# Zero matmuls ahead of the first data, and the identity loaded before the norm weights

## The chip, the cores and the metric

The kernel runs on one core of a Trainium2 chip. The metric is the time of one launch in microseconds (us), the median of three runs. The core has an engine for matrix products (TensorE, in the profile PE, and PEld for its loads of the stationary operand), three engines that work element by element (VectorE is DVE, ScalarE is ACT, GpSimd is POOL) and one that issues loads (SyncE, SP). Each has its own list of instructions and waits for the others on semaphores. Loads move data by 16 DMA engines which all queues share.

## The reference, cut to what matters

Four layers run one after the other over 256 tokens of width 2048, all in 32 bit floats: two hybrid layers, then a banded one and a grid one.

```python
def first_block(x, ...):
    for l in range(DEPTH):                       # DEPTH = 2
        x = hybrid_layer(x, pre_norm_g[l], post_norm_g[l], w_in[l], ...)
def hybrid_layer(x, pre_g, post_g, w_in, b_in, w_out, ...):
    h = rms_norm(x, pre_g)
    p = split_columns(h @ w_in + b_in)           # 2048 columns in, 6992 out
    ... four kinds of attention on the pieces of p ...
    return x + rms_norm(mix @ w_out, post_g)
def second_block(x, ...):
    x = _layer_ab(...); x = _layer_c(...)        # x + (attention(norm(x) @ w_in) * silu(z)) @ w_out
    return _rmsnorm(x, ln_f)
```

Only the very first product, `h @ w_in` of the first layer, is near the change. Its weights w_in are read from memory once, and nearly all of the kernel's TensorE time is spent in such products.

## The kernel before, in words

**Precision.** A product of 32 bit floats is made of three matmuls in the one-pass type fp32r: every operand is split in a high part (`w_hi`, `xt_hi`, written by ACT) and the rest (`w_lo`, `xt_lo`, written by DVE), and PE adds hi·hi, hi·lo and lo·hi. In the first slot these are lines 1552, 1553 and 1554, in all later ones 1503 to 1505.

**Chunks.** The columns of a weight matrix are worked off in slots of 512 columns. A slot has four chunks (0 to 3 for the first slot, 4 to 7 for the second, and so on), each of four pieces of 128 rows by 512 columns, 1 MB in all. Chunks go round a ring of three buffers `raw[0..2]`: SP loads a chunk when DVE has split the chunk that had the buffer before (`raw_free`, line 425), then ACT makes `w_hi` (line 641), DVE makes `w_lo` (line 975), then PE multiplies 24 matmuls.

**The start.** The first four chunks are worked piece by piece, since everything waits for data there. SP issues the first 256 columns of x, the pieces of chunk 0, and so on, x and pieces in turn (lines 432 and 435). ACT's queue issues two small loads: `gT`, the norm weights (line 854), and the identity matrix, which is the first 128 columns of `cst` (line 855). PE waits for the identity and the head of x, and transposes x (`x_cols_t(0)`, line 1535: four transposes into one bank of PSUM). ACT scales the turned columns by `gT` into `xt_hi` (lines 660 and 661), and splits two pieces (line 866). DVE writes `xt_lo` (line 1330) and `w_lo` (line 1322). Then `first_slot` starts: six matmuls of a piece, four transposes of the next columns of x (`x_cols_t(1)`), six matmuls, four transposes, and so on. From chunk 3 on, the ring decides when a load may be issued. SP also loads the rest of `cst` (line 448), and POOL, once that is in, the biases and small weights of the layer (lines 515 to 535) by its own queue.

**Order.** The order on each engine is written out by hand: the program of an engine is its instruction list. Nothing else decides it.

## Time and profile before

| | us |
|---|---|
| median of three runs | 1887.13 |
| the three runs | 1882.69, 1887.13, 1889.14 |
| the profiled execution, its own time | 1885.34 |
| its span, first to last instruction | 1883.3 |
| TensorE (PE) busy in it | 1857.6 |
| VectorE busy | 1011.1 |
| ScalarE busy | 859.5 |
| waits of PE for DVE's `w_lo` after the first slot, 5 times | 8.3 |
| wait of PE for the first data | 5.3 |

A row of the timeline gives the start, the duration, the engine, the line of the kernel, the operation, what it writes and reads with its shape, and in brackets how long the engine had been idle and what ended that. A row of the windows gives busy time of each engine in a stretch, then the clock that TensorE was granted as a share of its full 2.4 GHz (0.50 is 1.2 GHz), the busy share of the 16 DMA engines, and GB/s. The share can read slightly above 1. Before the first change of clock that the profiler recorded this column reads 1.00 in any case; there the distance between starts of equal matmuls tells the level.

### The profile page before, as it was taken

Reading aid. Unit: us, or ns where it says so; the run is one execution under the profiler, and the core shown is the slowest. Engines: PE = TensorE matmul, PEld = TensorE weight load, DVE = VectorE, ACT = ScalarE, POOL = GpSimd, SP = SyncE. Lnnn points to the kernel's source line nnn. Section 1 sums busy time; section 2 is a strip of 40 time slices with the busy share of each in tenths; the row PEclk is TensorE's granted clock in tenths of the full one; section 3 lists DMA queues with packets and bytes.
Section 4 is the critical chain, followed back from the end, with each engine's and each line's share of the span. In section 5 each row is a group of like instructions: output and inputs, shape, how many; then the busy total and the mean of one; then the engine's idle time right before and its main releaser. Section 6 shows DMA issues by size and latency. Waiting matters only on the chain.

```text
span 1883.3 us, 22540 instructions
## 1 busy us (share of the span) xinstructions
PE 1857.6 (99%) x9566; PEld 1590.7 (84%) x9566; DVE 1011.1 (54%) x987; ACT 859.5 (46%) x1066; POOL 163.2 (9%) x168
## 2 busy tenths in 40 slices
PE   8999999999999999999999999999999999999998
PEld 6889988898788998889878888888888888888886
DVE  5545454474663455457465555455455555555544
ACT  5344443464543445346445443354354434435443
POOL 2300011000340001000020000010000101100011
PEclk9999999999999999999999999999999999999999
DMA  9665555455566455446556555455556555456553
GB/s 313 201 193 153 157 189 169 145 182 190 191 203 205 144 172 191 149 140 205 170 176 197 183 192 189 161 184 175 182 179 200 179 167 184 146 172 201 174 184 112
DMA packets 187156, 338.99 MB, mean 180 GB/s; under 512 B 6848, under 2 KB 48688, under 8 KB 186160
## 3 DMA queue, kind: packets, MB, share of 16 engines
q1 hardware_dynamic: 181536, 316.89, 51.8%
q0 software_dynamic: 5232, 20.59, 3.9%
q8 instruction: 76, 1.25, 0.3%
q14 instruction: 24, 0.20, 0.0%
q10 hardware_dynamic: 288, 0.07, 0.0%
HBM read 335.43 MB, written 2.10 MB: 179 GB/s over the span
## 4 chain that ended last, share of the span: by engine, by line
PE 92%; DVE 3%; ACT 2%; DMA 1%; issue 1%; ACTq 0%; DVEq 0%
PE acc L1503 27%; PE acc L1505 27%; PE acc L1504 27%; PE bank L1656 3%; DVE w_lo L975 2%; PE bank L1596 1%; DMA raw<-in_w_in 1%; PE bank L1625 1%; PE bank L1645 1%; PE bank L1860 1%; PE bank L1586 1%; PE bank L1759 1%; ACT w_hi L641 1%; PE bank L1614 0%; DVE x L1299 0%
## 5 line engine op out<-in xcount | busy, mean ns | idle before, releaser
L975 DVE TENSOR_TENSOR w_lo<-raw,w_hi 128x2048 fp32r<-128x2048 f32 (+4 forms) x304 | 668.1, 2200 | 581.6 <-ACT w_hi L641 581.6
L1503 PE MATMUL acc<-w_hi,xt_hi 128*128 128x512 f32 (+4 forms) x2432 | 923.6, 380 | 8.5 <-DVE w_lo L975 8.3
L1505 PE MATMUL acc<-w_hi,xt_lo 128*128 128x512 f32 (+4 forms) x2432 | 915.7, 377 | 0.0
L1504 PE MATMUL acc<-w_lo,xt_hi 128*128 128x512 f32 (+4 forms) x2432 | 915.2, 376 | 0.0
L641 ACT ACTIVATE w_hi<-raw 128x2048 fp32r<-128x2048 f32 (+4 forms) x304 | 549.6, 1810 | 614.7 <-PE acc L1505 591.9
L1503 PEld LDWEIGHTS acc<-w_hi,xt_hi 128*128 128x128 f32 x2432 | 457.4, 188 | 89.4 <-DVE w_lo L975 7.0
L1505 PEld LDWEIGHTS acc<-w_hi,xt_lo 128*128 128x128 f32 x2432 | 457.3, 188 | 80.7
L1504 PEld LDWEIGHTS acc<-w_lo,xt_hi 128*128 128x128 f32 x2432 | 457.6, 188 | 78.7 <-issue 0.5
L716 ACT ACTIVATE S<-S,nmax 128x256 f32<-128x256 f32 (+1 forms) x128 | 59.9, 469 | 74.9 <-DVE nmax L1067 49.9
L515 POOL DMA_DIRECT2D bias<-in_b_in x32 | 18.0, 562 | 613.8 <-DVE M L1055 209.9
L703 ACT ACTIVATE PT<-bank 128x512 f32<-128x512 f32 (+2 forms) x76 | 36.3, 554 | 69.7 <-PE bank L1645 51.8
L615 POOL TENSOR_TENSOR side<-line,cst 128x512 f32<-128x512 f32 x16 | 25.8, 1647 | 457.2 <-DVE S L1072 457.2
L1111 DVE TENSOR_TENSOR M<-bank,rden 128x512 f32<-128x512 f32 x20 | 13.8, 692 | 41.5 <-PE bank L1656 41.5
L1656 PEld LDWEIGHTS bank<-TV,PT 128*128 128x128 f32 x288 | 33.5, 192 | 1.4 <-issue 0.8
L1656 PE MATMUL bank<-TV,PT 128*128 128x128 f32 x288 | 33.9, 275 | 0.5 <-DVE S L1267 0.5
L1072 DVE TENSOR_TENSOR S<-bank,side 128x512 f32<-128x512 f32 x32 | 21.8, 692 | 15.5 <-PE bank L1615 14.9
L703 ACT ACTIVATE QT_hi<-bank 128x512 fp32r<-128x512 f32 x16 | 8.7, 600 | 44.5 <-PE bank L1596 44.5
L1055 DVE SCALAR_TENSOR_TENSOR TQ<-acc,rinv,bias 128x512 f32<-128x512 f32 x16 | 11.3, 746 | 32.1 <-PE acc L1505 32.1
L1860 PE MATMUL bank<-raw,TV 128*15 128x128 f32 x256 | 28.3, 273 | 0.0
L1645 PE MATMUL bank<-cst,S 128*128 128x128 f32 x224 | 27.5, 274 | 0.4 <-ACT hid_rows L748 0.4
L1860 PEld LDWEIGHTS bank<-raw,TV 128*15 128x15 f32 x256 | 24.4, 96 | 4.0 <-issue 0.7
L1645 PEld LDWEIGHTS bank<-cst,S 128*128 128x128 f32 x224 | 25.1, 141 | 2.5 <-issue 1.0
(279 smaller groups left out, 1192.6 us busy)
## 6 DMA issues: line engine op xcount, KB each, us to landing
raw<-in_w_in SPq DMA_DIRECT2D x76, 1024.0 KB, 5.1
raw<-in_w_in_c SPq DMA_DIRECT2D x64, 1024.0 KB, 5.5
raw<-in_w_in_ab SPq DMA_DIRECT2D x52, 1024.0 KB, 5.1
raw<-in_w_out SPq DMA_DIRECT2D x32, 1024.0 KB, 5.1
raw<-in_w_out_ab SPq DMA_DIRECT2D x16, 1024.0 KB, 5.0
raw<-in_w_out_c SPq DMA_DIRECT2D x16, 1024.0 KB, 5.0
raw<-in_w_in SPq DMA_DIRECT2D x16, 688.0 KB, 4.0
raw<-in_w_in SPq DMA_DIRECT2D x16, 576.0 KB, 3.8
```

Of the source, the lines that this page charges most:

```text
L615: nc.gpsimd.tensor_tensor(table[:, h].rearrange("p t (k n) -> p t k n", n=GRID_W), shifted, c("na").unsqueeze(1).unsqueeze(1).broadcast_to ...
L641: nc.scalar.activation(w_hi[r][:, :, 0:n], raw[r][:, :, 0:n], ACT.Copy).then_inc(hi_done.s, 1)
L703: nc.scalar.activation(dst, src, ACT.Copy, scale=scale).then_inc(done.s, 1)
L716: nc.scalar.activation(s, s, ACT.Exp, bias=nmax[:, par, h, t:t + 1], accum_out=den[:, par, h, t:t + 1]).then_inc(u.probs.s, 1)
L975: nc.vector.tensor_tensor(w_lo[r][:, :, 0:n], raw[r][:, :, 0:n], w_hi[r][:, :, 0:n].bitcast(F32), ALU.subtract).then_inc(lo_done.s, 1)
L1072: nc.vector.tensor_tensor(S[:, h], bank[b][:, :].rearrange("p (t s) -> p t s", t=T), add(h), ALU.add).then_inc(u.biased.s, 1)
L1503: nc.tensor.matmul(s, xt_hi[:, kt, rows], w_hi[r][:, k, 0:n], start=(q == 0 and k == 0), stop=False)
L1504: nc.tensor.matmul(s, xt_hi[:, kt, rows], w_lo[r][:, k, 0:n], start=False, stop=False)
L1505: ins = nc.tensor.matmul(s, xt_lo[:, kt, rows], w_hi[r][:, k, 0:n], start=False, stop=(q == NQ - 1 and k == KQ - 1))
L1645: ins = nc.tensor.transpose(bank[b][:, to:to + P], flat(S, h)[:, at:at + P], ident)
L1656: ins = nc.tensor.matmul(bank[b][:, HD * h:HD * h + HD], flat(PT, h)[:, at:at + P], value(h, k), start=(k == 0), stop=(k == mine[-1][0]))
L1860: ins = nc.tensor.matmul(bank[v][0:N_CMP, 0:HD], blk[:, v, at, :], w[:, HD * j:HD * j + HD], start=(at == 0), stop=(at == CMP_LEN - 1))
```

## The change

Three things are done at the start of the program. ACT's queue issues the load of the identity first and that of the norm weights second. DVE writes zeros into the first 128 columns of `tmp`, ahead of its three small memsets. And PE, before it waits for the identity, does nine matmuls of these zeros by themselves into bank 3, and eight more behind `x_cols_t(0)`. Nobody reads their result; bank 3 is first used for data by `x_cols_t(3)`. The rest of the program is as it was; its line numbers are 2 higher (3 behind the new memset, 11 behind the second `keep_running`).

```diff
+IDLE_FIRST, IDLE_NEXT = 9, 8
...
+        zeros_set = signal("zeros_set", 0)
...
+            act.dma_start(cst[:, 0:P], const[:, 0:P]).then_inc(ident_in.s, 16)
             act.dma_start(gT[:, :], gains_t[0]).then_inc(gt_first.s, 16)
-            act.dma_start(cst[:, 0:P], const[:, 0:P]).then_inc(ident_in.s, 16)
             act.wait_ge(ident_in.s, 16)
...
+            nc.vector.memset(tmp[:, 0:P], 0.0).then_inc(zeros_set.s, 1)
             nc.vector.memset(spare[:, 0:1], 0.0).then_inc(lo_done.s, RING)
...
+            def keep_running(count):
+
+                for _ in range(count):
+                    nc.tensor.matmul(bank[3][:, 0:P], tmp[:, 0:P], tmp[:, 0:P], start=True, stop=True)
+
+            pe.wait_ge(zeros_set.s, 1)
+            keep_running(IDLE_FIRST)
             pe.wait_ge(ident_in.s, 16)
             x_cols_t(0)
+            keep_running(IDLE_NEXT)
```

PE's list at its start, with the semaphores that a row waits for; `bank<-cst,x` are the transposes of x, `acc` rows are the first slot. Before:

```order
L1479 UNCONDITIONAL_BRANCH [waits barrier_Pool_Activation_PE_DVE_SP_release]
L1535 MATMUL bank<-cst,x 128x128 [waits x_head,ident_in]
L1535 MATMUL bank<-cst,x 128x128 x3
L1552 MATMUL acc<-w_hi,xt_hi 128x512 [waits tr_lo,lo_piece,acc_out]
L1553 MATMUL acc<-w_lo,xt_hi 128x512
L1554 MATMUL acc<-w_hi,xt_lo 128x512
```

The same place of the changed kernel, where `bank<-tmp` are the products of zeros:

```order
L1831 MATMUL bank<-tmp 128x128 [waits zeros_set]
L1831 MATMUL bank<-tmp 128x128 x8
L1538 MATMUL bank<-cst,x 128x128 [waits x_head,ident_in]
L1538 MATMUL bank<-cst,x 128x128 x3
L1831 MATMUL bank<-tmp 128x128 x8
L1555 MATMUL acc<-w_hi,xt_hi 128x512 [waits tr_lo,lo_piece,acc_out]
L1556 MATMUL acc<-w_lo,xt_hi 128x512
```

Seventeen products were added, nine ahead of the first transpose and eight between it and the first real product; nothing changed places among the old ones.

ACT's list at its start, before:

```order
L854 DMA gT<-in_gains_t 128x16
L855 DMA cst<-in_const 128x128
L857 ACT_TABLE_LOAD
L857 ACTIVATE spare<-cst 128x1 [waits ident_in]
L660 ACTIVATE xt_hi<-bank,gT 128x256 [waits tr_full,gt_first]
```

And of the changed kernel:

```order
L856 DMA cst<-in_const 128x128
L857 DMA gT<-in_gains_t 128x16
L859 ACT_TABLE_LOAD
L859 ACTIVATE spare<-cst 128x1 [waits ident_in]
L662 ACTIVATE xt_hi<-bank,gT 128x256 [waits tr_full,gt_first]
```

The two loads have changed places; the first reader of `gT` is still the copy behind the transposes.

## Rows read from the trace of the kernel before

**Rows 1.** Page, part 1: busy time, share of the span, instructions.

```profile
PE 1857.6 (99%) x9566; PEld 1590.7 (84%) x9566; DVE 1011.1 (54%) x987; ACT 859.5 (46%) x1066; POOL 163.2 (9%) x168
```

**Rows 2.** Waits of PE, whole span: total us, times, longest.

```profile
PE acc L1503 <- DVE w_lo L975: 8.3, 5, 2.3
PE bank L1535 <- DMA cst<-in_const: 5.3, 1, 5.3
```

**Rows 3.** Timeline, ACT and its queue, first 18 us: start, duration.

```profile
0.81 0.45 ACTq L854 DMA_DIRECT2D gT<-in_gains_t  x1
1.29 0.49 ACTq L855 DMA_DIRECT2D cst<-in_const  x1
6.55 0.47 ACT L660 ACTIVATE xt_hi<-bank,gT 128x256 fp32r<-128x256 f32 x1 [1.04 <-PE bank L1535]
12.85 0.47 ACT L660 ACTIVATE xt_hi<-bank,gT 128x256 fp32r<-128x256 f32 x1 [4.42 <-PE bank L1535]
17.44 0.48 ACT L660 ACTIVATE xt_hi<-bank,gT 128x256 fp32r<-128x256 f32 x1 [0.69 <-PE bank L1535]
```

**Rows 4.** Timeline, PE, first 16 us.

```profile
5.33 1.12 PE L1535 MATMUL bank<-cst,x 128*128 128x128 f32 x4 [5.33 <-DMA cst<-in_const]
8.99 0.77 PE L1552 MATMUL acc<-w_hi,xt_hi 128*128 128x512 f32 x1 [2.55 <-DVE w_lo L1322]
9.56 0.63 PE L1553 MATMUL acc<-w_lo,xt_hi 128*128 128x512 f32 x1
9.98 0.63 PE L1554 MATMUL acc<-w_hi,xt_lo 128*128 128x512 f32 x1
...
13.25 0.39 PE L1554 MATMUL acc<-w_hi,xt_lo 128*128 128x512 f32 x1
13.48 0.40 PE L1552 MATMUL acc<-w_hi,xt_hi 128*128 128x512 f32 x1
...
15.25 0.50 PE L1552 MATMUL acc<-w_hi,xt_hi 128*128 128x512 f32 x1 [0.48 <-DVE w_lo L1322]
```

**Rows 5.** Loads issued in the first 2.2 us: size, us from issue to landing.

```profile
x<-in_x SPq DMA_DIRECT2D x1, 256.0 KB, 3.4
gT<-in_gains_t ACTq DMA_DIRECT2D x1, 8.0 KB, 3.3
...
cst<-in_const ACTq DMA_DIRECT2D x1, 64.0 KB, 4.0
```

**Rows 6.** Plain products of 128 columns in f32: busy us, mean ns.

```profile
L1656 PE MATMUL bank<-TV,PT 128*128 128x128 f32 x288 | 33.9, 275 | 0.5 <-DVE S L1267 0.5
```

**Rows 7.** Chain that ended last, 30 to 49 us: start, us.

```profile
32.01 11.71 DMA raw<-in_w_in
43.74 1.93 ACT w_hi L641
```

**Rows 8.** Windows: busy us of each engine, clock, DMA share, GB/s.

```profile
24.00:29.00 5.00, 5.00 (x28) 4.17 (x27) 2.67 (x6) 2.31 (x6) 4.74 (x9) 1.00 0.84 226
32.00:36.00 4.00, 4.00 (x19) 3.30 (x19) 2.29 (x1) 4.00 (x4) 0.00 (x0) 1.00 0.85 210
36.00:43.70 7.70, 7.70 (x36) 6.22 (x35) 4.43 (x8) 3.72 (x5) 0.00 (x0) 1.00 0.98 367
```

**Rows 9.** Timeline, PE, its longer idle times after the start.

```profile
49.16 0.50 PE L1503 MATMUL acc<-w_hi,xt_hi 128*128 128x512 f32 x1 [1.22 <-DVE w_lo L975]
...
501.13 0.80 PE L1503 MATMUL acc<-w_hi,xt_hi 128*128 128x512 f32 x1 [2.32 <-DVE w_lo L975]
...
982.37 0.76 PE L1503 MATMUL acc<-w_hi,xt_hi 128*128 128x512 f32 x1 [2.34 <-DVE w_lo L975]
```

**Rows 10.** Windows behind two of these idle times.

```profile
48.00:51.00 3.00, 1.84 (x8) 1.54 (x9) 3.00 (x2) 1.27 (x2) 3.00 (x1) 1.00 0.24 40
501.10:504.50 3.40, 3.37 (x8) 2.69 (x9) 3.36 (x11) 0.00 (x0) 2.02 (x3) 0.51 0.65 198
982.40:985.80 3.40, 3.40 (x8) 2.73 (x9) 3.36 (x11) 0.00 (x0) 2.08 (x3) 0.51 0.68 204
```

## The prediction

> **What bounds the kernel now.** I read the page's busy times first. PE is busy for 1857.6 of 1883.3 us [rows 1], so nearly all of the time is TensorE's work, which the change leaves alone. What a change at the start can touch is the little that PE is not busy, and the stretch in which it works at less than its full clock. The waits of PE come next: 5.3 us for the first data, and 8.3 us in five waits for `w_lo` later on [rows 2]. The last are in this argument because what is won in the first 20 us has to get past the first of them.
>
> The start itself is read from the timeline, ACT and PE side by side [rows 3, 4]. ACT's queue issues `gT` at 0.81 and the identity at 1.29 us; PE's transposes start at 5.33, released by the identity; ACT copies at 6.55, DVE splits, and the first real matmul starts at 8.99, 2.55 us after PE had gone idle. From there on matmuls of 512 columns start 0.42 us apart (9.56 to 9.98); from 13.25 on they start 0.23 us apart (13.25 to 13.48). That is TensorE at 1.2 GHz and then at 2.4 GHz. So the clock rose about 4 us behind the first real matmul; the four transposes before it had not been enough.
>
> **The change part by part.**
>
> *Identity first.* It takes 4.0 us from issue to landing, `gT` 3.3 and the head of x 3.4 [rows 5]. Issued at 0.81 the identity lands at 4.81 instead of 5.29: 0.48 us earlier. The head of x, issued at the same time as ACT's first load, has landed by 4.25 and doesn't take over. `gT`, now issued at 1.29, lands near 4.6; its reader, the copy at 6.55, moves to 6.07, so there is 1.5 us to spare. The term is −0.48 us for the start of the real chain, between 0 (the landing depends on what else the DMA engines have, not on the issue) and −0.48.
>
> *Nine products of zeros.* One plain f32 product of 128 columns costs 33.9 / 288 = 0.118 us at full clock [rows 6], so 0.236 at half. Nine take 2.1 us. They start when DVE's memset is through, about 1.1 us, and end at 3.2, well before the identity at 4.81. They cost nothing, also at the dearer price of 0.42 us each (the distance of the 512-column matmuls at half clock [rows 4]): 1.1 + 3.8 = 4.9, late by 0.1 us. The memset delays the three small ones behind it, of which one lets SP issue its first piece; SP issues x ahead of it, and that covers it.
>
> *Eight more.* The transposes go from 4.81; four take 4 × 0.22 = 0.9 us (their 1.12 us for first start to last end [rows 4] less what the last one overhangs). So PE is free for zeros from 5.7. At 0.236 they end at 7.6. The first real matmul is due at 8.99 − 0.48 = 8.51, so 0.9 us are to spare. At 0.42 each they end at 9.1, 0.6 us late. I take the first price, from 288 products of the same shape. Cost 0, bounds 0 and +0.6.
>
> *What the clock gives.* If PE is already at 2.4 GHz at 8.5 us, the stretch from the first real matmul to ACT's copy of the second transposes (8.99 to 12.85 = 3.86 us [rows 3, 4]) shrinks. The same sequence, six matmuls and four transposes, is there at full clock: from 15.25 to the copy at 17.44, 2.19 us. The difference is 1.67 us, and ACT's copies, DVE's splits and the matmul at 15.25 follow at once. What bounds this term: 0 if the clock still rises at 13, and 1.67. With the zeros PE has a hole of about 1.6 us before the identity and one of 0.9 before the real work, where it had 5.3 and 2.55; it is busy for 5 us before 8.5, longer than the 4 us from 8.99 to the rise, so I take all of it.
>
> By a rule of the Trainium skill (TensorE: Matmul & The Clock Gate, Part 1) the moment of the rise isn't tied to the kernel's start, and one kernel was measured with 6, 11 or 14 slow matmuls. In this trace the fully slow ones are six. With 0.2 us lost by each, the page would make the term 1.2 to 2.8 us instead of 1.67, changing from run to run.
>
> So PE, ACT and DVE run S = 0.48 + 1.67 = 2.15 us earlier from the third piece of chunk 0 on.
>
> *Where that goes.* PE is dense from 15.25 until 47.9, where it waits for chunk 6's `w_lo` until 49.16 [rows 9]. Behind this wait the chain is a load: chunk 6 was issued at 32.01, took 11.71 us for 1 MB, and ACT's split at 43.74 follows without a hole [rows 7]. The 16 DMA engines are at 0.98 from 36 to 43.7, with 367 GB/s [rows 8]; at that rate 1 MB takes 2.9 us, so chunk 6 stood in line for most of the 11.71. So issuing it 2.15 us earlier puts it in the same line. It lands earlier only by the holes that earlier issues fill. There are 5 × (1 − 0.84) = 0.8 us of them from 24 to 29, where chunk 5 was waiting to be issued (it waits for DVE and comes earlier now), and 4 × 0.15 = 0.6 us from 32 to 36 [rows 8], where chunk 6 was already issued, so that these don't fill. I take G = 0.8 us. The bounds are 0 (what is issued earlier only contends with POOL's small loads, which go when the rest of `cst` is in) and 2.15 (chunk 6's place in the line moves with its issue).
>
> After 49.16 nothing more is lost: loads are no longer in line, ACT and DVE are released by PE, and the later waits for `w_lo` hang on work that starts when PE allows it. So the shift at 49 us is the shift of the end. The wait at 47.9 itself grows, to 1.22 + 2.15 − 0.8 = 2.57 us.
>
> *The sum.* −0.8 us. The profiled execution took 1885.34 us, 1.8 us less than the median; the mean of it and the three runs is (1882.69 + 1885.34 + 1887.13 + 1889.14) / 4 = 1886.1, which I use as base since one execution of four is no better than another: 1886.1 − 0.8 = 1885.3 us. By the profiled execution alone it is 1884.5, by the median 1886.3.
>
> **The rivals.**
>
> *The clock falls in the longer wait (slower).* The waits of 2.32 and 2.34 us at 501 and 982 us are each followed by a stretch of 3.4 us at 0.51 of full speed [rows 9, 10]: 3.4 × 0.49 = 1.7 us lost. The wait of 1.22 us is not (1.00 in 48 to 51). The change lengthens that wait to 2.57 us, so it can trip the same thing: −0.8 + 1.7 = +0.9, 1887.0 us. It decides from somewhere between 1.22 and 2.32 us. For it: two waits of two of this length. Against it: those two are the only such cases, and if S or G is other than I took, the wait is shorter. Chance 0.27.
>
> *Chunk 6 moves by all of S.* Then −2.15: 1883.9 us, and the wait stays at 1.22. For it: the queue isn't at full GB/s from 24 to 36 (226 and 210 [rows 8]), so contention may thin out as well. Against: the share. Chance 0.13.
>
> *The zeros don't lift the clock.* Then only the 0.48 of the identity is left, of which chunk 6's landing takes over some 0.3: 1885.8 us. For it: after the transposes at 5.33 the clock stayed low for 7 us, and it rose in an unbroken run of matmuls, while the work with zeros has holes. Chance 0.17.
>
> *The eight stand in the way.* +0.6 less what the wait at 47.9 absorbs (all of it, as long as PE is early): about 0 to +0.6, 1886.4 us. Chance 0.03.
>
> **How the numbers follow.** Forecast 0.40, rivals 0.27, 0.13, 0.17, 0.03. All lie between 1883.9 and 1887.0, within 3.1 us; 0.3% is 5.7 us, about what a measurement of this kernel can tell from no change (its three runs lie 6.45 us apart). So no case by itself gives a time outside "same". What does is the scatter of a median of three, some 2 to 2.5 us to either side, on a base that may itself sit high: faster by over 0.3% needs under 1881.5, slower over 1892.8. Faster 0.06, same 0.91, slower 0.03. The range takes the cases and the scatter: 1882 to 1889 us.
>
> **What would show it right or wrong.** In the new profile: the identity's first reader and PE's transposes at 4.8 rather than 5.3; zeros from about 1.1 to 3.2 and 5.7 to 7.6; the first real matmul at 8.5; 512-column matmuls 0.23 apart from the first one on, and the copy of the second transposes at 10.7 instead of 12.85. Chunk 6's ACT split near 42.9 instead of 43.74, and a wait of PE of about 2.6 us that ends near 48.4; a clock of 0.5 behind it shows the slower rival. I am wrong if the real matmuls still start 0.42 apart, if the first of them comes later than 8.99, if chunk 6 lands 2 us earlier, or if the end moves by more than the shift at 49 us does, since I know of nothing behind it that the change reaches.

## The result, and the profile after

The changed kernel takes 1881.12 us (median of 8 runs, 1879.54 to 1882.64) beside 1885.82 us for the kernel before (8 runs, 1882.69 to 1889.14): 0.9973 of its time, 95% interval 0.9964 to 0.9983. That is 4.7 us faster, where I had forecast 0.8, and below the predicted range. The profiled execution took 1880.29 us, with a span of 1878.3; before it was 1885.34 and 1883.3. Ratios are of fast runs alone; the only slow ones anywhere are two of e2's twelve (3818.95 and 4943.6 us), and without them its median is 1882.72.

The start first, ACT (start, duration, engine, line, operation; in brackets the idle time and its releaser), answering to [rows 3]:

```profile
3.99 0.20 ACT L859 ACTIVATE spare<-cst 128x1 f32<-128x1 f32 x1 [0.89 <-DMA cst<-in_const]
6.22 0.47 ACT L662 ACTIVATE xt_hi<-bank,gT 128x256 fp32r<-128x256 f32 x1 [2.02 <-PE bank L1538]
10.82 0.47 ACT L662 ACTIVATE xt_hi<-bank,gT 128x256 fp32r<-128x256 f32 x1 [2.73 <-PE bank L1538]
```

The identity is in at 3.99, not at 4.81, but the copy behind the transposes moves only from 6.55 to 6.22. PE's timeline, answering to [rows 4], says why:

```profile
1.13 4.21 PE L1831 MATMUL bank<-tmp 128*128 128x128 f32 x18 [1.13 <-DVE tmp L1315]
5.13 0.98 PE L1538 MATMUL bank<-cst,x 128*128 128x128 f32 x4
5.95 1.95 PE L1831 MATMUL bank<-tmp 128*128 128x128 f32 x16
8.66 0.47 PE L1555 MATMUL acc<-w_hi,xt_hi 128*128 128x512 f32 x1 [0.77 <-DVE w_lo L1325]
8.97 0.39 PE L1556 MATMUL acc<-w_lo,xt_hi 128*128 128x512 f32 x1
9.20 0.40 PE L1557 MATMUL acc<-w_hi,xt_lo 128*128 128x512 f32 x1
...
13.22 0.50 PE L1555 MATMUL acc<-w_hi,xt_hi 128*128 128x512 f32 x1 [0.67 <-DVE w_lo L1325]
```

Nine products are 18 instructions: a plain f32 product is issued as two. They take 4.0 us and outlast both the identity and x (whose head had landed by 4.16). But they did what they are there for: the real matmuls are 0.23 us apart from the first one on (8.97 to 9.20), where they were 0.42 apart before. The profiler's first record of the clock's rise stands at 5.91 us; before it stood at 13.06. The third piece starts at 13.22 instead of 15.25, 2.03 us earlier. Of that, 0.33 us are already there at the first real matmul (8.66 for 8.99), and 1.70 come behind it.

This start isn't the same in every execution. Seven traces have nine and eight products of zeros (after, e14, e2, e4, e6, e7, e8); their first record of the rise lies between 4.80 and 7.17 us, and their third piece starts between 12.69 and 13.30. In e14, the same kernel once more, the first real matmul starts at 8.13 and the third piece at 12.69, 2.56 us earlier than before; the part behind the first real matmul is 1.70 there too. A difference of under half a microsecond between two traces of the start tells nothing by itself.

Then chunk 6, in the chain that ended last (start, us, what), answering to [rows 7]:

```profile
29.95 11.42 DMA raw<-in_w_in
...
41.40 1.93 ACT w_hi L643
...
43.35 3.71 DVE w_lo L977
...
47.10 0.50 PE acc L1506
```

It was issued 2.06 us earlier (29.95 for 32.01), took 11.42 us for 11.71, and ACT's split is 2.34 us earlier. Yet PE starts again only 2.06 us earlier (47.10 for 49.16), as DVE's `w_lo` took 3.71 us and before 3.43. This is DVE's row in the chain of before, and what POOL does meanwhile, before and after (the third of its operations on the columns that DVE has just written):

```profile
45.69 3.43 DVE w_lo L975
```

```profile
47.02 4.34 POOL L502 TENSOR_TENSOR TQ<-TQ,cst 128x1024 f32<-128x1024 f32 x1
```

```profile
44.97 4.35 POOL L504 TENSOR_TENSOR TQ<-TQ,cst 128x1024 f32<-128x1024 f32 x1
```

In both, `w_lo` ends 2.08 us behind the start of this operation (49.10 and 47.05). The experiments come back to it.

The windows of the same stretch (us, busy of PE, PEld, DVE, ACT and POOL, clock, DMA share, GB/s), the first two and the last answering to [rows 8, 10]:

```profile
24.00:29.00 5.00, 5.00 (x27) 4.14 (x27) 3.14 (x7) 4.01 (x9) 5.00 (x9) 1.00 0.99 341
32.00:36.00 4.00, 4.00 (x19) 3.30 (x18) 1.01 (x3) 3.97 (x7) 0.00 (x0) 1.00 0.88 315
29.00:32.00 3.00, 3.00 (x15) 2.49 (x14) 2.40 (x3) 3.00 (x2) 1.16 (x3) 1.00 0.55 84
48.00:51.00 3.00, 3.00 (x15) 2.48 (x14) 3.00 (x1) 0.00 (x0) 2.92 (x2) 1.00 0.66 183
```

The first two show 341 and 315 GB/s for 226 and 210; the third has 84 where the kernel before moves 376 GB/s in the same stretch. The weak stretch has changed place; over 24 to 36 us the kernel moves 3.2 MB, where before it moved 3.1.

PE's longer idle times after the start, answering to [rows 9]:

```profile
47.10 0.50 PE L1506 MATMUL acc<-w_hi,xt_hi 128*128 128x512 f32 x1 [1.23 <-DVE w_lo L977]
...
497.27 0.68 PE L1506 MATMUL acc<-w_hi,xt_hi 128*128 128x512 f32 x1 [2.35 <-DVE w_lo L977]
...
977.32 0.50 PE L1506 MATMUL acc<-w_hi,xt_hi 128*128 128x512 f32 x1 [2.33 <-DVE w_lo L977]
```

The wait at 47 us has the size it had, so everything behind it is 2.06 us earlier. But the distance grows on the way. Laying the starts of PE's instructions of the two traces side by side, the changed kernel is ahead by 2.06 us at 50, 1.92 at 220, 3.55 at 226, 3.51 at 480, 3.88 at 493, 5.01 at 599, and 5.04 from there to the end. So three places far from the edit gave another 3 us. The first is a stretch in which TensorE was granted half its clock, before (first row) and after (second):

```profile
221.30:224.60 3.30, 3.30 (x17) 3.30 (x17) 2.90 (x4) 0.46 (x2) 0.00 (x0) 0.50 0.25 45
```

```profile
221.00:224.40 3.40, 3.40 (x29) 3.40 (x29) 1.42 (x2) 2.60 (x9) 0.00 (x0) 1.00 0.28 50
```

The other two stand at 491 and at 588 to 599 us; the experiments come back to them.

### The profile page after: what moved, and what is told of

Its sections match the earlier page's. It is cut to its first block, busy times and chain, and to the rows that moved or that the text cites. A ratio compares the mean times of both kernels' runs of the same rounds, so it can differ in the third digit from the quotient of the medians.

```text
span 1878.3 us, 22609 instructions
## 1 busy us (share of the span) xinstructions
PE 1859.3 (99%) x9600; PEld 1593.4 (85%) x9600; DVE 1011.0 (54%) x988; ACT 859.5 (46%) x1066; POOL 163.2 (9%) x168
## 4 chain that ended last, share of the span: by engine, by line
PE 93%; DVE 3%; ACT 2%; DMA 1%; issue 1%; DVEq 0%; ACTq 0%
PE acc L1506 27%; PE acc L1508 27%; PE acc L1507 27%; PE bank L1659 3%; DVE w_lo L977 2%; PE bank L1599 1%; DMA raw<-in_w_in 1%; PE bank L1628 1%; PE bank L1648 1%; PE bank L1871 1%; PE bank L1589 1%; PE bank L1762 1%; ACT w_hi L643 1%; PE bank L1617 0%; DVE x L1301 0%
## 5 line engine op out<-in xcount | busy, mean ns | idle before, releaser
L1659 PE MATMUL bank<-TV,PT 128*128 128x128 f32 x288 | 33.9, 275 | 0.5 <-DVE S L1269 0.5
```

Of the source, the lines that this page charges most:

```text
L1659: ins = nc.tensor.matmul(bank[b][:, HD * h:HD * h + HD], flat(PT, h)[:, at:at + P], value(h, k), start=(k == 0), stop=(k == mine[-1][0]))
```

## The experiments

Times beside a run are of the kernel before in the same comparison where one is given. "Ahead by" is always how much earlier PE's instructions start than in the profiled execution of before.

### The two parts apart: e1, e2

e1 exchanges the two loads and does nothing else.

```diff
-            act.dma_start(gT[:, :], gains_t[0]).then_inc(gt_first.s, 16)
             act.dma_start(cst[:, 0:P], const[:, 0:P]).then_inc(ident_in.s, 16)
+            act.dma_start(gT[:, :], gains_t[0]).then_inc(gt_first.s, 16)
```

> The kernel before with only the two small loads exchanged, no zeros. Both theories see the identity at about 4.0 us (it landed at 3.97 with the change), the head of x at 4.2, so that PE's transposes start at 4.2 to 4.3 instead of 5.33 and everything up to 47 us is about 1.1 us earlier, with the clock still at half until some 12 to 16 us. Follow-the-issue theory (chunk 6 lands 11.4 to 11.7 us after its issue, whatever stands in the queue): its ACT split moves from 43.74 by the same 1.1 us, and the time is 1.1 us under the kernel before. Standing-in-line theory (landing moves by 0.8 of 2.15 of the shift): the split moves by 0.4 us. Rival on the change as a whole: if the exchange alone gives as much as the 2.0 us of the change, the zeros are worth nothing.

1884.73 us (1882.76 to 1888.15), ratio 0.9993, interval 0.9983 to 1.0004: no change that can be measured. PE's first work now waits for the other load:

```profile
4.83 1.09 PE L1535 MATMUL bank<-cst,x 128*128 128x128 f32 x4 [4.83 <-DMA x<-in_x]
8.47 0.76 PE L1552 MATMUL acc<-w_hi,xt_hi 128*128 128x512 f32 x1 [2.55 <-DVE w_lo L1322]
9.03 0.63 PE L1553 MATMUL acc<-w_lo,xt_hi 128*128 128x512 f32 x1
```

The transposes are 0.50 us earlier, the matmuls still at half clock (the last two rows, 0.56 apart, for 8.66 to 8.97 in the changed kernel), and at 48.57 PE is ahead by 0.58. Half a microsecond, but it isn't shown that the load order gave it: in e15 and e16, further down, the loads have the old order, the identity lands at 4.87 and 4.83 (5.29 in before), and the transposes start at 4.92 and 4.87. What the exchange does is seen in who ends the wait. In the new order the identity lands ahead of the head of x (4.50 and 4.70 here), and x takes over.

e2 has the zeros, with the loads in the old order.

> The changed kernel with the two loads in their old order (norm weights first). Theory: the nine products of zeros are 18 instructions that last until 5.3 us, longer than the identity needs in either order (3.97 or 5.28), so the exchange is worth nothing beside them: PE's transposes at 5.1 to 5.4, first real matmul at 8.6 to 8.8, time within 0.3 us of the changed kernel. Rival: the exchange carries its own 0.5 to 1.1 us, and this kernel is slower than the changed one by that.

1883.09 us, ratio 0.9978, interval 0.9968 to 0.9988. The nine products end at 5.3 us, when the identity lands at its old time anyway; the first real matmul starts at 8.48 and PE is ahead by 2.18 at 46.98. That lies between the 2.06 of the changed kernel and the 2.57 of e14. So the start's gain is there without the exchange, and beside nine products of zeros no gain of it can be seen.

### How many zeros, and of what size: e3, e5, e10, e11, e12

e3: six and five products, `IDLE_FIRST, IDLE_NEXT = 6, 5`.

> The changed kernel with 6 and 5 products of zeros instead of 9 and 8. At 0.234 us an instruction and two to a product, six end at 1.13 + 12 x 0.234 = 3.9 us, as the identity lands (3.97; head of x 4.16). The transposes start at 4.2 to 4.3 instead of 5.13, ACT's first copy at 5.3 instead of 6.22, the first real matmul at 7.7 instead of 8.66. Theory (the nine are too many, the clock still rises near 6 us): another 0.9 us, ratio to the kernel before about 0.9968. Rival (with fewer zeros the clock rises later, or the zeros behind the transposes run at half clock into the real work): real matmuls 0.42 us apart at first and no gain, or a loss up to 1 us, against the changed kernel.

1881.11 us, ratio 0.9972, interval 0.9960 to 0.9983. Its start:

```profile
1.13 2.93 PE L1831 MATMUL bank<-tmp 128*128 128x128 f32 x12 [1.13 <-DVE tmp L1315]
4.41 1.08 PE L1538 MATMUL bank<-cst,x 128*128 128x128 f32 x4 [0.36 <-DMA x<-in_x]
5.29 2.24 PE L1831 MATMUL bank<-tmp 128*128 128x128 f32 x10
8.04 0.47 PE L1555 MATMUL acc<-w_hi,xt_hi 128*128 128x512 f32 x1 [0.52 <-DVE w_lo L1325]
```

The zeros end before x lands (4.05 and 4.28), the real matmuls start at 8.04, and they are at full clock all the same. PE restarts at 46.55, ahead by 2.61 us. I had expected 0.9 us over nine and eight. Against the profile of the changed kernel it is 0.62 at the first real matmul and 0.55 at the restart, but against e14 it is 0.09 and 0.04. The third piece starts at 12.61 and 12.65 in the two traces with six and five (e3, e9), which is just ahead of the range of the seven with nine and eight (12.69 to 13.30). In the medians it doesn't show.

e5: products of one column by one, nine and eight of them.

```diff
-                    nc.tensor.matmul(bank[3][:, 0:P], tmp[:, 0:P], tmp[:, 0:P], start=True, stop=True)
+                    nc.tensor.matmul(bank[3][0:1, 0:1], tmp[:, 0:1], tmp[:, 0:1], start=True, stop=True)
```

> The changed kernel with its seventeen products shrunk to one row by one column: as many PE instructions, almost no work. The change moved the end by 5.04 us in the profile, of which 2.06 come from the start, 1.6 from a half-clock stretch that was at 221 us before, and some 1.5 from two places at 491 and 596 us. Fetch theory: PE's instructions are loaded 16 KB at a time by the same DMA engines, and the 68 more of them moved these loads; one fell into the load of the chunk behind the compress slot before (588.6 us, the chunk took 5.9 us) and none does after (4.7 us). Then this kernel has real matmuls 0.42 us apart at first, starts like the kernel with the two loads exchanged (third piece 0.5 us earlier than before), but is also 1 to 1.5 us better at 490 to 600 us: floor of its times 1.5 to 2 us under the kernel before. Rival (those 1.5 us come from the start, as a shift that changes what collides, or from chance): it equals the kernel with only the loads exchanged, whose lowest time is 0.4 us under before, and its chunk at 588 takes 5.8 us.

1883.04 us, ratio 0.9986, interval 0.9977 to 0.9995. The seventeen are over in 0.59 and 0.54 us. The first real matmul starts at 7.95, earlier than in e3, but at half clock: they start 0.42 us apart up to 12.35. PE is ahead by 1.06 at the third piece. The same number of instructions, over so soon, doesn't lift the clock.

e10: 64 of these small products ahead of the transposes and none behind (`IDLE_FIRST, IDLE_NEXT = 64, 0`).

> 64 one-by-one products before the identity and none behind, 256 instructions more on PE than before, which is one whole 16 KB load of instructions. They take some 4.2 us, until 5.3 us, so the start is as in the kernel before (transposes near 5.3, third piece within 0.3 us of 15.25), and the instruction loads stand where they stood there: one at 588 us. Fetch theory: the chunk behind the compress slot takes 5.8 us again and the chain of the changed kernels that won 0.4 at 491 and 1.1 us at 596 us loses that; lowest time near 1883.1 to 1883.6. Rival (the 1.5 us of the one-column kernel came from something else in the new code): the chunk takes 4.7 us and the lowest time is 1.5 us under before.

1883.61 us, ratio 0.9984, interval 0.9973 to 0.9996. They keep PE busy from 1.13 to 4.47; then it idles for 2.55 us before the first real matmul at 8.24, which is at half clock as well; the first record of a rise is at 11.12. Ahead by 1.13 at the third piece, where I had expected a start as before. It was meant for another question, and comes back under 588 us.

e11 and e12 have the nine alone and the eight alone.

> Nine products of zeros before the identity, none behind the transposes. Theory (the first nine, 4.2 us long, lift the clock by themselves near 6 us): the real matmuls start 0.23 us apart at 8.7 us, third piece at 13.2 us as in the changed kernel. Rival (the gap of 2.5 us behind the transposes, which the eight fill, keeps or drops the clock): 0.42 us apart until 12 us or so, third piece near 15.1.

> No products of zeros before the identity, eight behind the transposes. Transposes at 4.3 to 4.8, the eight from 5.2 to 8.9 at 0.234 us an instruction if the clock stays low, so that the first real matmul waits for them until 9.0 instead of 7.9. Theory: the clock rises only some 4 us behind 4.3 us, near 8 to 9 us; third piece 13.0 to 13.5 us, close to the changed kernel. Rival: it rises at 12 to 13 us as before, third piece near 15.

One run each, 1881.82 and 1887.11 us. The timeline of e11, and the window behind it:

```profile
1.13 3.74 PE L1831 MATMUL bank<-tmp 128*128 128x128 f32 x18 [1.13 <-DVE tmp L1315]
4.71 0.60 PE L1538 MATMUL bank<-cst,x 128*128 128x128 f32 x4
7.86 0.77 PE L1555 MATMUL acc<-w_hi,xt_hi 128*128 128x512 f32 x1 [2.55 <-DVE w_lo L1325]
8.42 0.63 PE L1556 MATMUL acc<-w_lo,xt_hi 128*128 128x512 f32 x1
```

```profile
7.70:11.00 3.30, 3.14 (x9) 2.48 (x10) 0.66 (x2) 0.00 (x0) 0.00 (x0) 0.50 1.05 403
```

The transposes run at full clock (0.60 us for four, as later in the kernel), as the clock was recorded at full from 4.24 to 7.66 us; it falls in the idle 2.55 us and is at half until 11.07. The nine lift it, the eight keep it. Ahead by 1.34 at the third piece. e12:

```profile
4.68 1.09 PE L1538 MATMUL bank<-cst,x 128*128 128x128 f32 x4 [4.68 <-DMA x<-in_x]
5.56 3.31 PE L1831 MATMUL bank<-tmp 128*128 128x128 f32 x16
8.63 0.48 PE L1555 MATMUL acc<-w_hi,xt_hi 128*128 128x512 f32 x1
```

The eight alone, at half clock, last until 8.87 and the clock is recorded at full from 8.40, just in time, so the start is ahead by 2.05 us, as much as in the profile of the changed kernel (2.03; 2.56 in e14). What makes its one run long comes far behind: a stretch of half clock at 595 us that is twice as long as the others (6.8 us) and a late chunk there. One run doesn't tell whether that belongs to it.

### Does chunk 6 stand in line: e7, e8, e4

e7 holds back the issue of chunk 6 until chunk 7's buffer would be asked for.

```diff
-                sp.wait_ge(*raw_free(turn, i))
+                sp.wait_ge(*raw_free(turn, i + 1 if turn == 0 and i == 6 else i))
```

> The changed kernel with the load of chunk 6 held until chunk 7 may be issued too, about 2.9 us later (32.9 instead of 29.95 us). Follow-the-issue theory (10.8 to 11.7 us from issue to landing in five kernels so far): it lands at 44 us instead of 41.4, PE's wait at 45.5 grows by 2.7 us. Standing-in-line theory: it lands where the line lets it, 41.4 to 42.5.

1880.17 us in one run. The chain:

```profile
32.86 8.96 DMA raw<-in_w_in
...
41.85 1.93 ACT w_hi L643
...
43.80 3.28 DVE w_lo L977
```

Issued 2.9 us later than in the changed kernel, it lands 0.45 us later. So the load does not follow its issue; it stands in line, as I had said. But PE restarts at 47.12, as without the hold (47.10): DVE's `w_lo` starts 0.45 us later and takes 0.43 us less. So the landing isn't what ends the wait. Here are seven traces side by side (us):

| | chunk 6 lands | `w_lo` starts | takes | POOL's third operation starts | `w_lo` ends | PE restarts |
|---|---|---|---|---|---|---|
| before | 43.71 | 45.69 | 3.42 | 47.02 | 49.10 | 49.16 |
| e5 | 41.33 | 43.30 | 4.78 | 46.01 | 48.08 | 48.13 |
| e2 | 40.61 | 42.59 | 4.33 | 44.84 | 46.92 | 46.98 |
| after | 41.37 | 43.35 | 3.70 | 44.97 | 47.05 | 47.10 |
| e7 | 41.82 | 43.80 | 3.27 | 44.99 | 47.07 | 47.12 |
| e14 | 41.74 | 43.71 | 2.82 | 44.45 | 46.53 | 46.59 |
| e6 | 42.48 | 44.46 | 2.31 | 44.69 | 46.77 | 46.82 |

Between e2 and e14 the load lands 1.13 us later and PE restarts 0.39 us earlier. In all fifteen traces that have this wait, `w_lo` ends 2.07 or 2.08 us behind the start of POOL's third operation, whenever it began; the same operation of DVE takes 2.29 us in e8, where POOL is idle beside it. POOL's first of these operations starts 0.93 or 0.94 us behind DVE's write of the columns that it reads, so it moves with the engines and not with the load. With it moves the whole gain of the start: the shift of the third piece and that of the restart agree within 0.05 us in each of the fourteen traces beside before (0.54 and 0.59 in e1, 1.06 and 1.02 in e5, 2.03 and 2.06 in after, 2.56 and 2.57 in e14). No run moves POOL's operations by themselves, so that they hold DVE back is read from the traces; that the landing doesn't end the wait is shown by e7.

e8 takes POOL's two large loads (`uq` and `ukv`, small weights of a later stage) out of the line and issues them behind slot 6; e4, run first, issued them behind slot 1.

```diff
-                nc.gpsimd.dma_start(uq, w_uq[...]...).then_inc(mlaw_in.s, 16)
-                nc.gpsimd.dma_start(ukv[:, :], flat(w_ukv)).then_inc(mlaw_in.s, 16)
...
                     next_bias(s)
+                    if s == 6:
+                        nc.gpsimd.dma_start(uq, w_uq[...]...).then_inc(mlaw_in.s, 16)
+                        nc.gpsimd.dma_start(ukv[:, :], flat(w_ukv)).then_inc(mlaw_in.s, 16)
```

> The changed kernel with POOL's loads of w_uq and w_ukv (1.1 and 0.5 MB) issued behind the second slot instead of at 28 us; nobody needs them before slot 11. Standing-in-line theory: chunk 6, issued at 29.9, then lands after the 3 to 6 us that 1 MB and its latency need, before 36 us instead of 41.4; PE's wait of 1.6 us between starts at 45.5 (1.3 us idle) goes, and the time falls by about 1.3 us against the changed kernel. Follow-the-issue theory: the landing stays 11.4 us behind the issue whatever else is loaded, 41.4 us, and the time stays.

> The changed kernel with POOL's loads of w_uq and w_ukv behind slot 6. Issued behind slot 1 they freed chunk 6 (PE's wait at 45.5 gone, 1.5 us won) but collided with chunk loads at 60 to 72 us, where a new wait of 1.3 us and more came. Behind slot 6 PE has slots of full length ahead. Theory: the 1.4 us stay won, ratio to the kernel before about 0.9966 against 0.9973. Rival: wherever these 1.6 MB go they hold a chunk back by as much, and the time equals the changed kernel's.

e4: 1881.98 us, ratio 0.9977, interval 0.9968 to 0.9985. The wait at 45 us is gone and PE ahead by 3.51 at 50, but a chunk load of 12.81 us then makes a new one:

```profile
76.61 0.50 PE L1506 MATMUL acc<-w_hi,xt_hi 128*128 128x512 f32 x1 [1.27 <-DVE w_lo L977]
```

Ahead by 1.24 at 100: the collision had only moved. e8: 1879.85 us (1879.48 to 1880.43), ratio 0.9968, interval 0.9957 to 0.9979. The wait is gone and stays gone; PE is ahead by 3.6 at 50 and at 480. In e8 chunk 6 lands at 35.04, and its `w_lo` is over at 40.07, ahead of POOL's operations; these then meet the `w_lo` of the next two chunks, and the first two of them take 2.42 and 3.33 us instead of 1.30 and 1.29. So, by these traces, the wait needs both: a line of 1 MB loads and POOL's loads that makes chunk 6 late by several microseconds, and POOL's operations, behind which its `w_lo` then comes to stand. Within the 3.1 us over which the landing varies in the other traces (40.61 to 43.71), it doesn't set the restart.

### The half-clock stretches: e6

e6 has PE multiply the identity by itself eight times ahead of each first slot, in the place of its wait at 494 and 975 us.

```diff
                 pe.wait_ge(*acc_out(turn, a - 1))
+                if order is FIRST_SLOT:
+                    for _ in range(8):
+                        nc.tensor.matmul(acc[a % 2][0][:, 0:P], ident, ident, start=True, stop=True)
```

> The changed kernel with eight products of the identity by itself, into the accumulator that the next product overwrites, at the start of the second, third layer, where PE waits 2.3 us for w_lo (494.6 and 974.7 us in the changed profile) and the clock is at half for 3.4 us behind each in most profiles. Theory: with PE busy for 1.9 of the 2.3 us the clock stays up, 1.7 us saved at each, up to 3.4 us, ratio to before about 0.9956. Rival: the clock falls for another reason, or the fillers delay the real ones: times as the changed kernel's or up to 1 us worse.

1879.64 us (1879.41 to 1879.88), ratio 0.9968, interval 0.9956 to 0.9981. The waits for `w_lo` in total, of the changed kernel and of this one:

```profile
PE acc L1506 <- DVE w_lo L977: 7.9, 5, 2.3
```

```profile
PE acc L1509 <- DVE w_lo L977: 5.5, 5, 1.2
```

The real matmuls start no earlier for it; the two longest waits are halved because the products fill a part. The two stretches at half clock behind them are gone, and only the one at 220 us is left. I had hoped for a ratio of 0.9956. The five runs lie within 0.5 us, all at a granted clock of 0.998, where the changed kernel's eight run from 0.995 to 0.997.

### What changed at 221, 491 and 588 us: e13 to e16

e13 and e14 are the two kernels as they are, once more; e15 is the kernel before with VectorE's clearing of `tmp` and nothing else; e16 is e5 with the loads in the old order, that is the kernel before with the clearing and 17 one-column products.

```diff
+            nc.vector.memset(tmp[:, 0:P], 0.0)
             nc.vector.memset(spare[:, 0:1], 0.0).then_inc(lo_done.s, RING)
```

> The kernel before, unchanged. If the half-clock stretch at 221 us, the wait of 0.18 us at 491 us and the late chunk load at 588 to 594 us (5.86 us from issue to split) belong to the kernel, all three come again, with PE restart 49.2 and a span of 1883 to 1885. If they change from execution to execution, one or more is missing and the span is 1 to 3 us shorter.

> The changed kernel, unchanged. If its lack of a stretch at 221 us is a property, it is lacking again and the span is 1878 to 1879. If it is chance, the stretch is there in this run and the span about 1.7 us longer; the chunk load of 588 us takes about 4.9 us by the instruction-fetch theory, since the fetches stand at 578.5 and 594.4.

> The kernel before with VectorE's clearing of tmp alone. If the 0.37 us at 491 us is won by TensorE's 34 more instructions, the trace has the wait of 0.18 us again; if by VectorE's one instruction, it is gone. PE restart at 49.2 as before either way; time as before, 1883 to 1887.

> Seventeen one-column products, loads in the old order. By the fetch theory TensorE's code stands as in e5 (fetch at 581 us), so the chunk load behind the compress slot takes 4.7 to 5.0 us; if the load order decides, it takes 5.9 as before. Third piece of the start about 1 us earlier than before; time 1881.5 to 1884.5.

One run each, beside 1888.35 us for the kernel before on that chip: e13 1888.38, e14 1879.37, e15 1883.25, e16 1881.83.

**221 us: chance.** e14, the changed kernel, has the stretch that it lacked, and lacks the one at 498 us, though the wait ahead of that is there (windows of e14; clock in the third column from the end):

```profile
219.90:223.20 3.30, 3.30 (x17) 3.30 (x17) 1.77 (x2) 0.73 (x2) 0.00 (x0) 0.50 0.22 36
498.10:501.50 3.40, 3.40 (x17) 2.81 (x18) 3.36 (x11) 0.00 (x0) 2.05 (x3) 1.00 0.69 225
```

e13, the kernel before, has two more than it had, at 598 and 707 us, and is 3.3 us longer. So a stretch is not a property of a kernel. Each costs about 1.7 us (3.41 us at half clock), and time goes with the granted clock: over 63 runs of the kernel before, taken beside the experiments, the mean is 1889.1 us at a granted clock of 0.994 (12 runs), 1887.3 at 0.995 (13), 1885.9 at 0.996 (19) and 1884.2 at 0.997 (18); one is at 0.992 and took 1893.5.

**491 us: one instruction more on VectorE.** DVE in the kernel before, then in e15:

```profile
483.50 0.15 DVE L989 TENSOR_SCALAR newton<-stat 128x1 f32<-128x1 f32 x1
484.26 0.16 DVE L980 RECIPROCAL stat<-stat 128x1 f32<-128x1 f32 x1 [0.60 <-ACT stat L697]
```

```profile
481.81 0.15 DVE L989 TENSOR_SCALAR newton<-stat 128x1 f32<-128x1 f32 x1
482.20 0.16 DVE L980 RECIPROCAL stat<-stat 128x1 f32<-128x1 f32 x1 [0.24 <-ACT stat L697]
```

The reciprocal comes 0.76 us behind its forerunner in the one and 0.39 in the other, though the square root of ACT between them ends in both at the same distance. Those 0.37 us reach PE as a wait for `xt_lo` at 491.72. The fifteen traces with the memset have 0.40 us there, and before, e13 and e1, without it, 0.76. The gain is not the zeros' and not TensorE's. That the memset at the start takes it away is shown. Why DVE stops there is open; that it hangs on how many instructions stand before is a guess.

**588 us: more instructions on TensorE.** This is the load of the first chunk behind the compress slot of the second layer, on the chain of waits before (first) and after:

```profile
587.06 6.26 DMA raw<-in_w_in
...
593.34 1.92 ACT w_hi L641
```

```profile
583.21 5.10 DMA raw<-in_w_in
...
588.33 1.92 ACT w_hi L643
```

From ACT's operation on `hid_rows`, which stands just ahead on its queue (587.48 us in before), to the split of the chunk it is 5.86, 6.03, 6.03 and 5.99 us in before, e13, e15 and e1, whose TensorE list is the old one, and 4.70, 4.72 and 4.94 us in after, e14 and e16, whose list is 34 matmul instructions longer. The other kernels that are 34 longer (e2, e4, e5, e7, e8) have 4.74 to 4.96 us, and those with 22, 54 and 66 more (e3, e9, e6) 5.00, 4.67 and 4.97. e15 and e16 differ in nothing but those products and the semaphore ahead of them, so it is not the load order, nor VectorE's one instruction. What stands in the trace beside it is a load on the queue for instructions, while the chunk is under way (queues in 587 to 593.4 us of before: packets, MB, share):

```profile
q8 instruction: 1, 0.02, 1.2%
```

The four kernels of about 6 us have it 1.1 to 1.2 us behind the start of `hid_rows`; those of 5.00 us and less have it 4.1 us and more ahead of that. e10 (128 more) has it 0.6 us behind, and takes 5.4 us to the split, 0.5 us less than before, where I had expected 5.8; e11 (18 more) and e12 (16 more) have it 3.6 us ahead, and take 5.76 and 7.36, which the load of code doesn't explain. One packet of 16 KB that takes a microsecond of one DMA engine's time is little for a delay of 1.1 to 1.3 us, so the load of code is a companion and not shown as the cause. That TensorE's longer list takes the 1.1 us away is shown by e15 and e16, one execution each, and borne out by the others; it isn't a matter of more or less alone, since 16, 18 and 128 more give none of it or half.

### All three together: e9

Six and five zeros, POOL's loads behind slot 6, and the filled waits.

> Six and five products of zeros, w_uq and w_ukv behind slot 6, and the filled waits at the two layer starts, together. Each alone: fewer zeros 0.5 us earlier at the third piece, the late weights 1.5 us at 47 us, the filled waits two half-clock stretches of 1.7 us (their times lie within 0.5 us of each other, where the changed kernel's spread over 3). If they add up, 1.5 + 0.5 us under the filled waits' 1879.6, about 1877.7, ratio to before near 0.9957. Rival: the late weights and the filled waits were measured at 0.9968 each, 0.9973 the change itself, so a good part may be the same thing, and the sum is no better than 0.9965.

1877.39 us (1877.16 to 1878.93), ratio 0.9949, interval 0.9937 to 0.9961. It is faster than the changed kernel by 3.7 us between the medians, and the two intervals don't meet (that of the changed kernel begins at 0.9964). The waits for `w_lo`, answering to [rows 2]:

```profile
PE acc L1510 <- DVE w_lo L978: 4.0, 4, 1.1
```

## Why the prediction was wrong

**What bounds the kernel, right.** PE is busy for 1859.3 of 1878.3 us after, 1.7 more with the zeros in, and the whole gain came out of idle time and slow clock.

**Identity first, near in size, wrong in its reason.** −0.48 forecast for the start and −0.50 in e1, but that is luck in one trace: with no lasting zeros ahead of them the transposes start at 4.31, 4.68 and 4.83 in the new order (e5, e12, e1) and at 5.33, 5.37, 4.92 and 4.87 in the old (before, e13, e15, e16), half a microsecond apart in the mean with a scatter as large. I had written that the head of x "doesn't take over"; it does, in each trace of the new order where PE waits. And I added the 0.48 to the zeros, and it was not to be had beside them.

**The price of the zeros, wrong by a factor of two.** I divided 33.9 us by the 288 of [rows 6]. Those are instructions, and a plain f32 product is two: at half clock it costs 4.0 / 9 = 0.44 us, not 0.236. Nine last until 5.13, past the identity. The bound of 0.42 that I had worked out from the 512-column matmuls was near it, and I took the other. It cost 0.3 us for the transposes (5.13 for 4.81) and 0.15 for the first real matmul (8.66 for 8.51).

**What the clock gives, right.** 1.67 us forecast; 1.70 measured behind the first real matmul, in the profile after and in e14 alike. The third piece moved by 2.03 and 2.56 where I had 2.15 with the identity's share. Full clock from the first real matmul held, and so did the copy near 10.7 (10.82). The rival that the zeros don't lift the clock fell, with e11 and e12 as its two halves: either group by itself runs long enough to lift it, but only one that reaches close to the real work keeps it. By a rule of the Trainium skill (TensorE: Matmul & The Clock Gate, Part 1) the count of slow matmuls changes from run to run. The trace agrees: before has six matmuls at half clock ahead of its second transposes and one behind, e13 has six and three (the rise is recorded at 13.06 and 14.22). It doesn't change the third piece, 15.25 and 15.28, as its wait takes it up.

**The step that failed: where S goes, G = 0.8.** I took chunk 6's landing for what ends the wait at 47.9, since the chain leads back through ACT's split to that load, and let only what the line of loads gives, G = 0.8 of S = 2.15 us, pass on to PE. The path was wrong. PE moved by 2.06 us, all of S, and the wait kept its size (1.23 us for 1.22). The wait ends with DVE's `w_lo`, and that ended 2.08 us behind the start of POOL's third operation in before, in after and in every other trace with the wait; with the load held back (e7) the landing was 0.45 us later and the restart the same. POOL's operations follow the engines, so all of S passes, in each of fourteen traces. Even by my own G little would have been lost: `w_lo` began 1.33 us ahead of POOL's third operation in before, and in e6 it was in time with 0.23; by these rows the load had an estimated 1.1 us to spare.

The size of G was off as well. ACT's split, behind the landing, came 2.34 us earlier, where I had 0.8 from the busy share of 24 to 29 us. The GB/s of the same row had room for more: at 226 of some 370 there are 5 × (1 − 226/370) = 1.9 us. But neither reading gives the landing in general: it comes 0.06 to 3.1 us earlier than before in the other thirteen traces with the wait, 3.1 in e2 and 1.23 in e6 with nearly the same start. Nor were it small packets that made the share high and the rate low: they are 2.1 KB on average in 24 to 29 us before and 2.0 after (1.13 MB in 538 and 1.71 MB in 846). What made them slow stays open.

The rival "chunk 6 moves by all of S" has the shift right (−2.15, and a wait of 1.22), to which I gave 0.13. Its reason, that the place in the line moves with the issue, is refuted by e7; that its number came true is luck.

**The slower rival, fell with G.** The wait did not grow, so nothing tells what 2.57 us would have done there; the clock behind it is 1.00 in 48 to 51 us. In e11 an idle time of 2.55 us is followed by half clock; in e14 one of 2.3 us isn't.

**"After 49.16 nothing more is lost", wrong.** 0.37 us at 491 and 1.1 us at 588 came by instructions that stand elsewhere in their lists (e13 to e16). This is the second step that failed: I put everything behind 49 us at nothing, knowing of nothing there that the change reaches, and 1.5 us came from there.

**The sum.** 2.06 + 0.37 + 1.1 = 3.5 us can be placed. At equal granted clock the difference is 1884.2 − 1879.9 = 4.3 us (0.997; 18 and 4 runs), 1885.9 − 1882.0 = 3.9 (0.996; 19 and 2 runs) and 1887.3 − 1882.5 = 4.8 (0.995; 13 and 2 runs), and between the medians it is 4.7. So some 0.4 to 1.3 us isn't placed; up to 0.5 of it can be the start, which gave 2.57 in e14. In the two profiles, 5.04 us apart, 1.6 us are that the changed kernel's met one stretch of half clock fewer; whether the change makes them rarer stays open. The base was not at fault: 1886.1, where the 63 runs have a mean of 1886.4. The chances took 0.3% as out of reach since every case lay within 2.2 us of the base.

## What to carry to other kernels

Where TensorE waits for its first data, give it products of zeros up to the first real matmul, sized to end just before each datum lands: here six and five plain f32 products of 128 columns, each worth two instructions. The eight behind the transposes gave as much by themselves and the nine ahead of them didn't, in one trace each (e12, e11).

A chain that leads back to a load doesn't say that the load decides. Look at how long the last operation took beside its usual time, and at which other engine's operation its end keeps a fixed distance from, in several traces; then hold the load back and see whether anything moves.

Before a gain of a few tenths of a per cent is put down to an idea, run the kernel with the same number of instructions and without the idea, and run both kernels again: here 1.5 of 4.7 us came from that, and two executions of one kernel have a start that differs by 0.5 us.

## What was not expected of the hardware

- A plain f32 product of 128 by 128 by 128 is two matmul instructions, 0.22 us apart at 1.2 GHz (18 of them in 4.0 us).
- The clock rises and falls again within the start: full from 4.24 to 7.66 us in e11, then half until 11.07. TensorE had been idle from 5.31 to 7.86.
- VectorE's `w_lo` takes 2.3 to 4.8 us beside GpSimd's operations at 44 to 51 us (2.29 in e8, with GpSimd idle), and in fifteen traces ends 2.07 or 2.08 us behind the start of the third of them. GpSimd's first two take 1.30 and 1.29 us in those, and 2.42 and 3.33 in e8.
- Stretches of 3.4 us at half clock come at a few places that the kernels share (near 220, 500, 600, 702 and 980 us), each in some executions and not in others; in e10 and e12 one of them is 6.8 us long. Those near 500 and 980 follow a wait of 2.3 us (29 of the 32 such waits in the sixteen traces other than e6 and e9 are followed by one), the ones near 600 one of 1.4 us (1.9 in e12), and those near 220 and 702 stand behind 8 us without a wait.
- One VectorE instruction more at the start takes 0.37 us away at 491 us, and 34 on TensorE take 1.1 us away at 588.
